# One block for projections, search and attention: splitting, rotation and search moved into the attention steps

## The chip, the cores and the metric

The kernel runs on one core of a Trainium2 chip. A time is device microseconds (us) of one execution, from launch to end. The profile comes from one profiled execution of its own; its span runs from the first instruction to the last.

## The reference

One decoder layer on 1024 tokens with 16 meta tokens in front of them (T = 1040), width 1024. All of it is float32.

```
proj = rms_norm(h) @ w_in                      # q,k,v of both attentions, index q,k,w, two gates
stick-breaking, 8 heads of 64, strictly causal:
  z = q k^T / 8;  log_not = -softplus(z);  a = exp(log_sigmoid(z) + sum of log_not over later keys);  o = a v
selected attention, 8 heads of 64, q and k rotated on their first 16 columns:
  score = sum over 8 index heads of relu(q_idx k_idx^T) * w_idx      # index q,k rotated on 8 of 32 columns
  the 256 highest-scored visible keys per query; softmax over them;  o = p v
merged = sigmoid(g_sb + b) * (o_sb @ w_branch_sb) + sigmoid(g_ds + b) * (o_ds @ w_branch_dsa)
h = h + rms_norm(merged @ w_out);  h = h + rms_norm(relu(rms_norm(h) @ w1)^2 @ w2)
```

## The kernel before

Every float32 matrix product is made of three reduced ones: each operand is split into `hi` (a copy in the fp32r type) and `lo` (what is left), and hi*hi, lo*hi and hi*lo are added in PSUM. Weights come in 123 units of 1024 x 128. For a unit, the SP queue loads `w_raw`, ACT makes `w_hi` (L120), POOL makes `w_lo` (L124), and PE multiplies 8 slices by 3 products over 1040 columns as three banks of 348, 348 and 344 columns, or over 1024 as two of 512 (`unit_mm`, L138).

The kernel is a row of blocks, with all engines meeting between them.

- **Norm** (L152 to L258): x is normalised, transposed and split into `x_hi`, `x_lo`.
- **Projections and search** (L345 to L675): 43 units, index units first, then 24 units of q, k, v and 16 of gates. ACT evacuates each (L425, L427, L475) and SP stores it unsplit to DRAM. Index rows come back, DVE rotates them (`rotate`, L557), they go out and come back four times over, ACT and POOL split them (L447, L494). From unit 9 on PE does one index head per unit between its slices (L548), through two one-bank buffers; ACT applies relu (L461) and DVE accumulates into `sc` (L588). Then DVE alone finds the 256th highest score of every query: 31 bits, highest first, and for each bit one counting pass over each of 7 key lengths (272 to 1040, L637), a comparison (L641) and a predicated copy (L644), and after it the mask `sel` (L655 to L675). PE multiplies the remaining units meanwhile. The q and k of the selected attention are rotated on DVE after the search, through DRAM.
- **Attention** (L722 to L1047): 128 jobs, one for each of 8 heads, 2 kinds and 8 blocks of 128 queries, with 144 to 1040 keys. They run as 4 turns of a hardware loop with 32 jobs each; a head of the stick-breaking kind (SB) and one of the selected kind (DS) alternate, longest block first. Operands come back from DRAM; DVE rounds q and k (L1034, L1035) and POOL makes their rest (L776, L778). A job: PE makes the logits (L824, L825, for SB also the mask, L827). SB: ACT takes two sigmoids (L901, L905), DVE scans (L980) and multiplies (L983). DS: DVE adds the mask and finds the extreme (L998), ACT takes the exponential (L908) and scales (L926). Then PE transposes the weights (L845), ACT rounds them (L920), DVE makes the rest (L1016), PE multiplies by v (L858), and ACT and DVE split the output (L932, L1029). Each engine's program fixes which job's part comes next; a job passes through some five of these steps.
- **Branches** (8 units), then **output product, norms and MLP**.

Of the kernel before, what the change touches and what calls it, by code (L numbers as in the profile page):

```python
# [7 lines left out]

# [35 lines left out]
U_IDX, U_QKV, U_GATE, U_BRANCH, U_OUT, U_MLP = 0, 3, 27, 43, 51, 59  # L44
# [13 lines left out]
R_V, R_K, R_Q = [0, 1536], [512, 2048], [1024, 2560]  # L58
R_GATE = 3072
# [7 lines left out]
O_MAIN = O_SEL + 2 * sum(KEYS)  # L67
O_RB = O_MAIN + 4 * NB * 1024


def key_chunks(n):

    return [(c, min(c + HALF, n)) for c in range(0, n, HALF)]


def build(nc, x, meta, w_units, b_gate, g_pre, g_post, g_mlp_pre, g_mlp_post, ident, strict, fill,
          rope_i, rope_d, out):
    with ExitStack() as ctx:
# [46 lines left out]

        def slot(base, i, k):

            return i * 2 + (base + k), (base + k) % 2, i + (base + k) // 2
# [132 lines left out]
        SB, DS = 0, 1  # L261
        O_RAW = O_MAIN + 2 * T * 4 + 2 * 8192
        q_raw = at("q_raw", [P, SEQ], F32, O_RAW)
        k_raw = at("k_raw", [P, T], F32, O_RAW + SEQ * 4)
        v_raw = at("v_raw", [DH, T], F32, O_RAW + (SEQ + T) * 4)
        unit_in = sem("a_in")

        def fetch(sp, hd, t):

            for half in range(2):  # L270
                sp.dma_start(q_raw[64 * half:64 * half + 64], proj[ds(hd * DH + R_Q[t], DH), META:T]).then_inc(unit_in, 16)
                sp.dma_start(k_raw[64 * half:64 * half + 64], proj[ds(hd * DH + R_K[t], DH), :]).then_inc(unit_in, 16)
            sp.dma_start(v_raw[:], proj[ds(hd * DH + R_V[t], DH), :]).then_inc(unit_in, 16)


        o = O_MAIN
        stage = at("stage", [P, 2, T], F32, o); o += 2 * T * 4
        qi_raw = at("qi_raw", [P, 2, SEQ], F32, o); o += 8192
        qi = at("qi", [P, 2, SEQ], F32R, o); o += 8192
        ki_raw = at("ki_raw", [P, T], F32, o); o += T * 4  # L280
        ki = at("ki", [P, T], F32R, o); o += T * 4
        relu_b = at("relu_b", [P, 2, HALF], F32, o); o += 4096
        sc = at("sc", [P, STOT], F32, o); o += STOT * 4
        junk2 = at("junk2", [P, 2, T], BF16, o); o += 2 * T * 2
        rp = [at(f"rope{n}", [P, T], F32, o + n * T * 4) for n in range(6)]
        o += 6 * T * 4
        rp_cos = at("rp_cos", [P, T], F32, o); o += T * 4
        rp_sin = at("rp_sin", [P, T], F32, o); o += T * 4
        w_tok = at("w_tok", [P, NB * HI], F32, o); o += 256
        w_t = at("w_t", [HI, SEQ], F32, o); o += SEQ * 4  # L290

        st_bits = at("st_bits", [P, 64], F32, o); o += 256
        assert o <= O_END, o
        sc_top = at("sc_top", [P, STOT], BF16, O_MAIN + 2 * T * 4)
# [3 lines left out]
        bit, need, thr = st_bits[:, 49:50], st_bits[:, 50:57], st_bits[:, 57:64]  # L298
# [10 lines left out]
        with ExitStack() as st:  # L309
# [22 lines left out]
            def _(sp):  # L332
# [19 lines left out]
                def stream(base, n, ahead=None):  # L352
                    with sp.Fori(0, n // 2) as i:
                        for k in range(2):
                            u, s, use = slot(base, i, k)
                            if ahead:
                                ahead(i, k)
# [1128 lines left out]
```

## Time and profile before

| | us |
|---|---|
| median of 3 runs | 2070.76 |
| lowest, highest | 2070.5, 2075.63 |
| the profiled execution | 2083.67 |
| its span | 2081.8 |
| PE busy | 1842.7 (89%) |
| DVE busy | 1106.9 (53%) |
| ACT busy | 700.2 (34%) |
| POOL busy | 465.1 (22%) |

The busy shares are averages over stages with different limits, so the span is cut into windows at the places where the work changes. "PEclk" is the TensorE clock that was granted, as a share of full speed. In a timeline, each row is the start, the time from the first start to the last end of the instructions merged in it, the engine, line, operation and tiles, and in brackets the idle time before it with what ended it.

### The profile page before, as it was taken

How to read it: one execution, taken by the hardware profiler on the slowest of the kernel's cores; microseconds unless marked ns; L12 is line 12 of the kernel's file. 1: busy time of each engine (PE TensorE's matmuls, PEld its weight loads, DVE VectorE, ACT ScalarE, POOL GpSimd, SP SyncE). 2: the span in 40 equal slices, each digit the busy share in tenths (PEclk: the TensorE clock that was granted, in tenths of full speed). 3: DMA queues.
4: the chain of work that ended last, by engine and by line, in shares of the span. 5: the costliest groups of instructions: out<-in, count | busy, mean ns of one | idle time of the engine just before them, and what ended most of it. 6: DMA issues, size and time to landing. Idle time of an engine off the chain costs nothing. (4 is left out here: it accounts for less than half of the span.)

```text
span 2081.8 us, 28389 instructions
## 1 busy us (share of the span) xinstructions
PE 1842.7 (89%) x10297; PEld 1573.4 (76%) x10297; DVE 1106.9 (53%) x1898; ACT 700.2 (34%) x1243; POOL 465.1 (22%) x186
## 2 busy tenths in 40 slices
PE   4988889999965877768778998999999999999997
PEld 3987889988754666656657786888888888888885
DVE  5106569999996768867778432442222222222226
ACT  4123442122113666656656413240302213021122
POOL 0124232122122202110111145021403214032230
PEclk7998889999987888878878999999999999999998
DMA  4232122242133121112212145321202112021123
GB/s 132 98 128 81 62 70 92 91 136 97 40 121 87 27 54 42 37 33 47 48 32 52 62 140 197 107 71 41 81 11 71 41 41 74 10 79 33 48 68 135
DMA packets 43405, 151.83 MB, mean 73 GB/s; under 512 B 6384, under 2 KB 6768, under 8 KB 43296
## 3 DMA queue, kind: packets, MB, share of 16 engines
q1 hardware_dynamic: 43296, 150.35, 23.1%
q8 instruction: 72, 1.18, 0.3%
q14 instruction: 37, 0.30, 0.1%
HBM read 117.81 MB, written 32.52 MB: 72 GB/s over the span
## 5 line engine op out<-in xcount | busy, mean ns | idle before, releaser
L138 PE MATMUL u_ps<-x_hi,w_hi 128*128 128x348 f32 (+1 forms) x904 | 226.1, 352 | 33.1 <-POOL w_lo L124 19.9
L124 POOL TENSOR_TENSOR w_lo<-w_raw,w_hi 128x1024 fp32r<-128x1024 f32 x53 | 129.2, 2439 | 477.7 <-ACT w_hi L120 477.7
L138 PE MATMUL u_ps<-x_lo,w_hi 128*128 128x348 f32 (+1 forms) x904 | 223.1, 348 | 0.0
L138 PE MATMUL u_ps<-x_hi,w_lo 128*128 128x348 f32 (+1 forms) x904 | 222.7, 348 | 0.0
L1339 ACT ACTIVATE relu<-bank 128x1024 f32<-128x1024 f32 x32 | 32.9, 1029 | 504.7 <-PE bank L1250 504.7
L1250 PE MATMUL bank<-m_hi,w_hi 128*128 128x512 f32 x512 | 199.5, 390 | 0.0
L1250 PE MATMUL bank<-m_hi,w_lo 128*128 128x512 f32 x512 | 199.2, 389 | 0.0
L1250 PE MATMUL bank<-m_lo,w_hi 128*128 128x512 f32 x512 | 199.2, 389 | 0.0
L138 PEld LDWEIGHTS u_ps<-x_hi,w_hi 128*128 128x128 f32 x904 | 163.9, 196 | 45.1 <-ACT stage L475 20.3
L845 PE MATMUL tp<-idf,a_buf 128*128 128x128 f32 (+1 forms) x704 | 124.3, 311 | 81.8 <-DVE pt_lo L1016 42.7
L1218 POOL TENSOR_TENSOR w_lo<-w_raw,w_hi 128x1024 fp32r<-128x1024 f32 x32 | 82.9, 2597 | 403.7 <-ACT w_hi L1315 403.7
L138 PEld LDWEIGHTS u_ps<-x_lo,w_hi 128*128 128x128 f32 x904 | 163.5, 196 | 11.9
L138 PEld LDWEIGHTS u_ps<-x_hi,w_lo 128*128 128x128 f32 x904 | 161.3, 193 | 11.4
L1420 DVE TENSOR_TENSOR acc<-acc,bank 128x1024 f32<-128x1024 f32 x56 | 68.3, 1220 | 188.4 <-PE bank L1226 187.6
L858 PE MATMUL o_ps<-pt_hi,v_hi 128*64 128x128 f32 (+1 forms) x704 | 159.2, 248 | 4.8 <-DVE o_lo L1029 3.5
L1407 DVE TENSOR_TENSOR sq<-relu 128x1024 f32<-128x1024 f32 x32 | 39.2, 1225 | 227.9 <-ACT relu L1339 227.9
L845 PEld LDWEIGHTS tp<-idf,a_buf 128*128 128x128 f32 (+1 forms) x704 | 78.5, 144 | 100.8 <-DVE pt_lo L1016 51.0
L1016 DVE TENSOR_TENSOR pt_lo<-tp,pt_hi 128x512 fp32r<-128x512 f32 (+3 forms) x224 | 121.8, 570 | 51.8 <-ACT pt_hi L920 50.4
L858 PE MATMUL o_ps<-pt_lo,v_hi 128*64 128x128 f32 (+1 forms) x704 | 149.1, 234 | 0.0
L858 PE MATMUL o_ps<-pt_hi,v_lo 128*64 128x128 f32 (+1 forms) x704 | 148.2, 233 | 0.0
L776 POOL TENSOR_TENSOR q_st<-q_raw,q_st 64x1024 fp32r<-64x1024 f32 x17 | 40.1, 2359 | 432.3 <-DVE k_hi L1035 432.3
L920 ACT CAST pt_hi<-tp 128x512 fp32r<-128x512 f32 (+3 forms) x224 | 104.3, 494 | 93.1 <-PE tp L845 92.8
(188 smaller groups left out, 3964.6 us busy)
## 6 DMA issues: line engine op xcount, KB each, us to landing
w_raw<-w_units SPq DMA_DIRECT2D x99, 512.0 KB, 3.5
proj<-stage SPq DMA_DIRECT2D x24, 520.0 KB, 2.7
raw<-w_units SPq DMA_DIRECT2D x24, 512.0 KB, 3.4
k_raw<-proj SPq DMA_DIRECT2D x34, 260.0 KB, 5.0
q_raw<-proj SPq DMA_DIRECT2D x34, 256.0 KB, 4.5
proj<-stage SPq DMA_DIRECT2D x16, 512.0 KB, 2.7
gate<-proj SPq DMA_DIRECT2D x16, 512.0 KB, 3.9
v_raw<-proj SPq DMA_DIRECT2D x17, 260.0 KB, 5.7
```

What stands on the lines that cost most here:

```text
L124: pool.tensor_tensor(w_lo[:, s], w_raw[:, s], w_hi[:, s].bitcast(F32), ALU.subtract).then_inc(lo_done, 1)
L138: mm = pe.matmul(o, w[:, s, kt, :], a[:, a_of(kt), c0:c1], start=(kt == kts[0] and n == 0), stop=(kt == kts[-1] and n == 2))
L776: pool.tensor_tensor(q_st[64:P, s], q_raw[64:P], q_st[64:P, s].bitcast(F32), ALU.subtract).then_inc(unit_lo, 1)
L845: mm = pe.transpose(tp[q][0:r, m * P:(m + 1) * P], a_buf[:, j % 4, c * P:c * P + r], idf[:])
L858: mm = pe.matmul(ops[s][0:DH, 0:P], v[0:r, t, c, :], w[0:r, s, c, :], start=(m == 0 and k_ == 0), stop=(m == len(tiles) - 1 and k_ == 2))
L920: act.copy(pt_hi[:, s, 4 * g:4 * g + m, :], tp[q][:, 0:m * P].rearrange("p (c k) -> p c k", c=m)).then_inc(rounded, 1)
L1016: dve.tensor_tensor(pt_lo[dst], tp[q][:, 0:m * P].rearrange("p (c k) -> p c k", c=m), pt_hi[dst].bitcast(F32), ALU.subtract).then_inc(b_fr ...
L1218: pool.tensor_tensor(unit_lo(v), raw_ring[(v - V0) % 3], unit_hi(v).bitcast(F32), ALU.subtract).then_inc(lo_done, 1)
L1250: mm = pe.matmul(m1_ps[n][:, c * HALF:(c + 1) * HALF], w[s][:, kt, :], a[:, kt, c * HALF:(c + 1) * HALF], start=kt == 0 and i == 0, stop=k ...
L1339: act.activation(relu8[:], m1_ps[n][:], ACT.Relu).then_inc(relu_done, 1)
L1407: dve.tensor_tensor(sq[:], relu8[:], relu8[:], ALU.mult).then_inc(sq_done, 1)
L1420: dve.tensor_tensor(acc[:, t], acc[:, t], m2_ps[g][:], ALU.add).then_inc(acc_done, 1)
```

## The change

- The projection block, the search and the attention block become one block, and their hardware loops become straight code. `CHUNK` lists 104 chunks: a unit's 348, 348 or 344 columns, or 512, each in one PSUM bank of its own pair.
- The rows of q and k are regrouped in the weights on the host, so that both halves of a rotation lie in one unit (`iA`, `rq`, `rk`). Rotation happens when such a chunk is evacuated: ACT copies it with its halves swapped, DVE multiplies twice and adds. Every q and k chunk is split at evacuation (ACT `stage_hi`, DVE `stage_lo`) and stored as hi and lo, so the rounding on ACT and DVE and the rests on POOL behind each reload go.
- 11 units are multiplied first, with the 8 index heads dealt between their slices (`INDEX_AT`) over four one-bank buffers. The other 32 units are dealt over the 64 SB jobs (`FILL`), by a table of costs that gives each step the same PE work.
- The attention steps run through all 64 SB jobs first and then all 64 DS jobs; blocks alternate between long and short (`BLOCKS`). The step of DVE holds two parts of the search (`SEARCH`): they are drawn from a generator, `select()`, that yields a cost in ns behind every instruction, until the sum of these has reached what the table has made due. The table shares 300,000 ns over 62 steps.
- The search reads the float32 scores in all 31 bits (before, the upper 15 bits came from a bf16 copy). The scan is done in place. The scaling by the softmax's sum moves from ACT (L926) to DVE (a `tensor_scalar`). Logits go to banks of at most 512 columns.
- SB outputs are stored to DRAM and come back, four pairs of heads, during the DS jobs (`RELOAD`), since `x_hi` and `x_lo` hold their place until then.
- In the branch block a gate is loaded as soon as its buffer is free, no longer behind the previous merge.

```diff
+BLOCKS = (7, 0, 6, 1, 5, 2, 4, 3)
+JOBS = [(t, H * t + h, i) for t in (SB, DS) for h in range(H) for i in BLOCKS]
...
+def work(j):
+    keys = [KEYS[JOBS[x_][2]] if 0 <= x_ < NJ else 0 for x_ in (j, j - 2, j - 3)]
+    return 0.89 * keys[0] + 0.9 * keys[1] + 1.41 * keys[2]
+
+def dve_work(j):
+    return (3.42 * KEYS[JOBS[j - 1][2]] if j >= 1 else 0) + (1.33 * KEYS[JOBS[j - 2][2]] if j >= 2 else 0) + 250
...
+cost_ = lambda n: 3 * (CHUNK[n][2] - CHUNK[n][1]) * 0.4435
...
+SEARCH_STEPS = STEPS - 2
+SEARCH_NS = 300e3
+dve_step = (SEARCH_NS + sum(dve_work(j_) for j_ in range(SEARCH_STEPS))) / SEARCH_STEPS
+SEARCH = [[max(0.0, dve_step - dve_work(j_)) / 2] * 2 if j_ < SEARCH_STEPS else [0.0, 0.0] for j_ in range(NJ + 4)]
+SEARCH[SEARCH_STEPS] = [1e8, 0.0]
...
             @block.tensor
...
+                for j in range(NJ + 3):
+                    if j < NJ:
+                        scores(j)
+                    for n, kt in FILL[j][0]:
+                        project(n, kt)
+                    if 2 <= j < NJ + 2:
+                        turn(j - 2)
...
+                    for n, kt in FILL[j][1]:
+                        project(n, kt)
+                    if j >= 3:
+                        product(j - 3)
...
             @block.vector
...
+                def select():
...
+                    for bit in reversed(range(BITS)):
+                        op(dve.tensor_scalar(cand.bitcast(I32), cur.bitcast(I32), 1 << bit, None, ALU.bitwise_or))
+                        yield 100
+                        settle()
+                        for j, b in enumerate(range(1, NB)):
+                            op(dve.tensor_scalar(sel[:, BOFF[b]:BOFF[b] + KEYS[b]], sc[:, blk(b)], cand[:, j:j + 1], None, ALU.is_ge, ALU.add,
+                                                 accum_out=cnt[:, j:j + 1]))
+                            yield 60 + 1.05 * KEYS[b]
+                        settle()
+                        op(dve.tensor_tensor(keep, cnt, thr_n, ALU.is_ge))
+                        yield 100
+                        settle()
+                        op(dve.copy_predicated(cur, keep.bitcast(I32), cand))
+                        yield 100
+                        settle()
...
+                for j in range(NJ + 4):
+                    if 4 <= j and JOBS[j - 4][0] == DS:
+                        rest_output(j - 4)
+                    if 1 <= j < NJ + 1:
+                        if JOBS[j - 1][0] == SB:
+                            stick(j - 1)
+                        else:
+                            normalise(j - 1)
+                    if j < NJ and JOBS[j][0] == DS:
+                        logits(j)
+                    if j < NJ + 3:
+                        for n in ENDS[j][0]:
+                            rest(n)
+                    due += SEARCH[j][0]
+                    while spent < due:
+                        spent += next(search, 1e9)
+                    if 2 <= j < NJ + 2:
+                        rest_weights(j - 2)
...
+                    due += SEARCH[j][1]
+                    while spent < due:
+                        spent += next(search, 1e9)
```

The first place is DVE in the search. Before, this is the loop's end, with nothing but the search in it (`sc` holds the scores, `st_bits` the bits, counts and thresholds):

```order
L637 TENSOR_SCALAR junk_364,st_bits<-sc,st_bits 128x784
L636 REGISTER_ALU
L637 TENSOR_SCALAR junk_364,st_bits<-sc,st_bits 128x912
L636 REGISTER_ALU
L637 TENSOR_SCALAR junk_364,st_bits<-sc,st_bits 128x1040
L639 TENSOR_SCALAR st_bits<-st_bits 128x1
L640 REGISTER_ALU
L641 TENSOR_TENSOR st_bits<-st_bits 128x7
L642 REGISTER_ALU
L644 COPY_PREDICATED st_bits<-st_bits 128x7
```

Now one step of DVE, in the fourth SB head (L949 and L952 are the scan and product of a job, L836 a chunk's `stage_lo`, L989 the rest of the transposed weights; L892, L896, L899 and L888 are the search):

```order
L949 SCALAR_TENSOR_TENSOR n_buf<-n_buf 128x528
L952 TENSOR_TENSOR a_buf<-a_buf,n_buf 128x528
L836 TENSOR_TENSOR stage_lo<-bk,stage_hi 128x512
L892 TENSOR_SCALAR sel,st_bits<-sc,st_bits 128x912
L892 TENSOR_SCALAR sel,st_bits<-sc,st_bits 128x1040
L989 TENSOR_TENSOR pt_lo<-bk,pt_hi 128x512
L989 TENSOR_TENSOR pt_lo<-bk,pt_hi 128x256
L896 TENSOR_TENSOR st_bits<-st_bits 128x7
L899 COPY_PREDICATED st_bits<-st_bits 128x7
L888 TENSOR_SCALAR st_bits<-st_bits 128x7
L892 TENSOR_SCALAR sel,st_bits<-sc,st_bits 128x272
L892 TENSOR_SCALAR sel,st_bits<-sc,st_bits 128x400
```

A bit's counts are now cut by the work of two jobs and a chunk, and one bit takes about a step.

The second place is where the search ends on DVE, in the step that holds the scan of job 45 (row one is its product; L940 is the last instruction of `select()`):

```order
L952 TENSOR_TENSOR a_buf<-a_buf,n_buf 128x400
L940 TENSOR_TENSOR sel<-sel,fill_f 128x128 x8
L989 TENSOR_TENSOR pt_lo<-bk,pt_hi 128x512
L989 TENSOR_TENSOR pt_lo<-bk,pt_hi 128x384
L949 SCALAR_TENSOR_TENSOR n_buf<-n_buf 128x656
L952 TENSOR_TENSOR a_buf<-a_buf,n_buf 128x656
L989 TENSOR_TENSOR pt_lo<-bk,pt_hi 128x512
L949 SCALAR_TENSOR_TENSOR n_buf<-n_buf 128x528
L952 TENSOR_TENSOR a_buf<-a_buf,n_buf 128x528
```

The search thus lies in steps 0 to 46 of the 64; in steps 47 to 63 DVE has only the jobs' own work.

The third place is PE in an attention step. Before (L845 transposes weights, L824 to L827 make logits, L858 multiplies by v):

```order
L845 MATMUL tp<-idf,a_buf 128x128 x7
L845 MATMUL tp<-idf,a_buf 16x128
L824 MATMUL z<-k_hi,q_st 128x400
L825 MATMUL z<-k_lo,q_st 128x400
L827 MATMUL z<-strict_b,idb 128x128
L858 MATMUL o_ps<-pt_hi,v_hi 64x128
```

Now (L647 multiplies by v, L622 to L625 make logits, L574 is a projection slice; `bk` are the eight PSUM banks):

```order
L647 MATMUL bk<-pt_hi,v_hi 64x128
L647 MATMUL bk<-pt_lo,v_hi 64x128
L647 MATMUL bk<-pt_hi,v_lo 64x128
L622 MATMUL bk<-k_hi_361,q_st_359 128x328
L623 MATMUL bk<-k_lo_363,q_st_359 128x328
L622 MATMUL bk<-k_hi_361,q_st_359 128x328
L623 MATMUL bk<-k_lo_363,q_st_359 128x328
L625 MATMUL bk<-strict_b,idb 128x128
L574 MATMUL bk<-x_hi,w_hi 128x348
```

Between the logits and the transposes of a step, and again behind the transposes, PE now has projection slices: 3 to 8 of them each time, in all 64 SB steps and in none of the DS steps.

## Rows read from the trace of the kernel before

**Rows 1.** Windows by stage: bounds, length, busy time of each engine, clock, DMA share.
```profile
45.00:150.00 105.00, 104.77 (x656) 104.49 (x656) 13.12 (x8) 16.96 (x25) 20.02 (x8) 0.98 0.35 115
150.00:161.00 11.00, 2.96 (x9) 2.53 (x9) 0.15 (x1) 4.29 (x6) 9.25 (x4) 0.56 0.12 48
161.00:305.00 144.00, 122.58 (x620) 114.79 (x621) 91.21 (x95) 60.48 (x123) 51.35 (x22) 0.84 0.24 74
305.00:628.00 323.00, 301.95 (x1541) 266.97 (x1539) 295.75 (x688) 68.31 (x81) 63.94 (x26) 0.97 0.27 95
628.00:643.00 15.00, 1.19 (x9) 0.94 (x9) 3.09 (x7) 1.78 (x4) 6.55 (x3) 0.54 0.49 124
643.00:1170.00 527.00, 406.63 (x3488) 340.04 (x3488) 397.16 (x815) 333.35 (x736) 86.01 (x33) 0.85 0.19 42
1170.00:2082.00 912.00, 886.16 (x3904) 730.29 (x3904) 282.32 (x248) 190.40 (x231) 223.11 (x86) 0.99 0.22 75
```

**Rows 2.** Timeline of PE: the first projection and the first branch product.
```profile
45.12 1.21 PE L138 MATMUL u_ps<-x_hi,w_hi 128*128 128x348 f32 x3 [6.31 <-PEq L147]
1170.53 0.72 PE L138 MATMUL br<-o_hi,w_hi 128*128 128x512 f32 x2 [1.49 <-PEq L722]
```

**Rows 3.** PE at full clock: two timeline rows, then one of the chain (start, length).
```profile
259.37 0.64 PE L138 MATMUL u_ps<-x_hi,w_hi 128*128 128x348 f32 x3
259.85 0.64 PE L138 MATMUL u_ps<-x_lo,w_hi 128*128 128x348 f32 x3
...
1411.57 43.77 PE bank L1226 x192
```

**Rows 4.** DVE in the index scores (timeline), and POOL's two groups beside it.
```profile
178.59 7.81 DVE L588 SCALAR_TENSOR_TENSOR sc<-relu_b,w_tok,sc 128x272 f32<-128x272 f32 x4 [2.99 <-ACT relu_b L461]
...
L124 POOL TENSOR_TENSOR w_lo<-w_raw,w_hi 128x1024 fp32r<-128x1024 f32 x53 | 129.2, 2439 | 477.7 <-ACT w_hi L120 477.7
L494 POOL TENSOR_TENSOR qi<-qi_raw,qi 32x1024 fp32r<-32x1024 f32 x16 | 39.1, 2443 | 1.7 <-POOL w_lo L124 1.0
```

**Rows 5.** Timeline of DVE in the search: its ends, and two bits.
```profile
313.44 1.50 DVE L597 TENSOR_TENSOR sc<-sc,fill_f 128x128 f32<-128x128 f32 x7 [0.29 <-DVE sc L588]
...
406.86 2.15 DVE L644 COPY_PREDICATED st_bits<-st_bits 128x7 f32<-128x7 int32 x1
409.39 0.17 DVE L632 TENSOR_TENSOR st_bits<-st_bits 128x7 int32<-128x7 int32 x1 [0.39 <-DVE st_bits L644]
...
415.75 0.17 DVE L644 COPY_PREDICATED st_bits<-st_bits 128x7 f32<-128x7 int32 x1
416.30 0.17 DVE L632 TENSOR_TENSOR st_bits<-st_bits 128x7 int32<-128x7 int32 x1 [0.39 <-DVE st_bits L644]
...
624.14 2.57 DVE L674 TENSOR_TENSOR sel<-sel,fill_f 128x128 bf16<-128x128 bf16 x8
```

**Rows 6.** DVE's groups for the jobs (count, busy us, mean ns, idle before), three by shape.
```profile
L1016 DVE TENSOR_TENSOR pt_lo<-tp,pt_hi 128x512 fp32r<-128x512 f32 (+3 forms) x224 | 121.8, 570 | 51.8 <-ACT pt_hi L920 50.4
L980 DVE TENSOR_TENSOR_SCAN c_buf<-n_buf 128x1040 f32<-128x1040 f32 (+3 forms) x64 | 98.2, 1534 | 31.2 <-ACT n_buf L905 30.9
L983 DVE TENSOR_TENSOR a_buf<-a_buf,c_buf 128x1040 f32<-128x1040 f32 (+3 forms) x64 | 66.1, 1033 | 2.2
...
L980 DVE TENSOR_TENSOR_SCAN c_buf<-n_buf 128x656 f32<-128x656 f32 x8 | 21.8, 2724 | 0.0
L980 DVE TENSOR_TENSOR_SCAN c_buf<-n_buf 128x784 f32<-128x784 f32 x7 | 12.5, 1781 | 0.0
L983 DVE TENSOR_TENSOR a_buf<-a_buf,c_buf 128x656 f32<-128x656 f32 x8 | 23.2, 2904 | 0.3
L983 DVE TENSOR_TENSOR a_buf<-a_buf,c_buf 128x784 f32<-128x784 f32 x7 | 6.8, 975 | 0.2
```

**Rows 7.** DVE scaling in place by a per-row scalar, 7 lengths of 272 to 1040.
```profile
L619 DVE TENSOR_SCALAR sc<-sc,st_bits 128x272 f32<-128x272 f32 (+6 forms) x7 | 3.9, 562 | 0.2
```

**Rows 8.** Waits in the attention stage: total us, times, longest.
```profile
ACT L900 <- PE z L827: 27.5, 3, 9.3
```

More of the change, by code:

```diff
@@ L9 @@
+import itertools
 from contextlib import ExitStack
@@ new lines, with even_chunks @@
+LO_NO = {n: k for k, n in enumerate(n for n in range(NC_ALL) if UNITS[CHUNK[n][0]][0] not in ("v", "g"))}
+CPU = {"iA": LAST_CHUNK[0] + 1}
+STORES = []
+for n_ in range(NC_ALL):
+    kind_ = UNITS[CHUNK[n_][0]][0]
+    dmas_ = {"iA": 8, "iC": 4, "rq": 4, "rk": 4, "v": 1, "g": 1}.get(kind_, 2)
+    STORES.append(dmas_ + (STORES[n_ - 2] if n_ >= 2 else 0))
+def even_chunks(keys):
+    n = -(-keys // HALF)
+    step = -(-keys // (2 * n)) * 2
+    return [(c * step, min((c + 1) * step, keys)) for c in range(n)]
@@ new lines @@
+STEPS = NJ // 2
+left_ = [(n_, k_) for n_ in range(NC_STEP, NC_ALL) for k_ in range(KT)]
+cost_ = lambda n: 3 * (CHUNK[n][2] - CHUNK[n][1]) * 0.4435
+per_step = (sum(cost_(n_) for n_, _ in left_) + sum(work(j_) for j_ in range(STEPS))) / STEPS
+FILL, due_, spent_ = [], 0.0, 0.0
+for j_ in range(NJ + 3):
+    parts_ = []
+    for part_ in range(2):
+        if j_ < STEPS:
+            due_ += (per_step - work(j_)) / 2
+        got_ = []
+        while left_ and j_ < STEPS and (spent_ < due_ or (j_ == STEPS - 1 and part_ == 1)):
+            got_.append(left_.pop(0))
+            spent_ += cost_(got_[-1][0])
+        parts_.append(got_)
+    FILL.append(parts_)
@@ L285, in build @@
[L285 to L294, printed above, removed]
+        stage_hi = at("stage_hi", [P, 2, HALF], F32R, O_STAGE)
@@ L520, in stream @@
-                def stream(base, n, outs, between=None):
-                    with pe.Fori(0, n // 2) as i:
-                        for k in range(2):
-                            u, s, _ = slot(base, i, k)
-                            unit(u, s, outs(s), before=between and (lambda kt: between(i, k, kt)))
-                for u in range(3):
-                    unit(u, u % 2, OUTS(u % 2))
-                stream(3, 6, OUTS)
-                pe.wait_ge(wt_in, 16)
-                for i in range(NB):
-                    mm = pe.transpose(sps[0][:, i * HI:(i + 1) * HI], w_t[:, i * P:(i + 1) * P], idf[0:HI, 0:HI])
@@ new lines, in logits @@
+                def logits(j):
+                    t, g, i = JOBS[j]
+                    s, keys = j % 2, KEYS[i]
+                    last = 3e38
+                    if j - 2 < NJ // 2:
+                        dve.wait_ge(a_done, j - 1)
+                    else:
+                        dve.wait_ge(exp_done, j - 1 - NJ // 2)
+                    for m, (c0, c1) in enumerate(ZCH[i]):
+                        z = Z_END[j] - len(ZCH[i]) + m
+                        dve.wait_ge(z_ready, z + 1)
+                        if m:
+                            dve.wait_ge(zd_used, z - NZ_SB)
+                        out = small[:, 16 + s:17 + s] if c1 == keys else small[:, 18 + m:19 + m]
+                        dve.tensor_tensor_reduce(n_buf[:, s, c0:c1], bk[(2 + z - NZ_SB) % 4][:, 0:c1 - c0], sel[:, BOFF[i] + c0:BOFF[i] + c1],
+                                                 -DH ** -0.5, last, ALU.add, ALU.min, out).then_inc(zd_used, 1)
+                        last = out
```

1380 lines of the change are left out of this document (676 added, 704 removed).

## The prediction

> **What bounds the kernel now.** I read the windows by stage first [rows 1]. Behind 1170 us PE is busy for 886 of 912 us at a clock of 0.99; nothing of the change reaches that part but the gate loads, which PE never waits for there. So everything lies between the first projection at 45.1 us and the first branch product at 1170.5 us [rows 2], 1125 us. The reader should see that no engine is full in them: PE is busy nearly throughout 45 to 150, but idle for 8 of the 11 us to 161, at 0.84 of the clock up to 305, and in the attention stage (527 us) PE is busy 77% at a clock of 0.85, DVE 75%, ACT 63%. From 305 to 628 PE and DVE are both near full: projections beside the search. The attention stage is bounded by hand-offs between three engines, the rest by PE or by DVE in turn. A merged stage can gain by filling PE's gaps with projections and DVE's with the search; what it cannot go below is the sum of work on the fuller engine.
>
> **PE's rates.** Three 348-column products start 0.48 us apart from the next three, so one takes 0.158; 192 products of 512 take 43.77, so 0.228 each [rows 3]. A unit of three banks is 72 x 0.158 = 11.4 us, one of two 48 x 0.228 = 10.9 us. Attention on PE is 406.6 us of busy time at 0.85 for 16 heads [rows 1]: 406.6 x 0.85 / 16 = 21.6 us a head at full clock, 2.7 us a job.
>
> **First 11 units with the index heads.** 7 units of three banks and 4 of two are 80 + 43 = 123 us. The 104 index products add about 0.2 us each, an estimate just above the 348-column price: 21 us. Before, a head took 20.5 us beside an 11.4 us unit, since POOL split q in two instructions of 2.44 us and DVE's accumulations stood still beside them: four of 272 columns took 7.81 us [rows 4]. That splitting now goes, and four buffers stand for two. What is late next is the first index operand: index q and k must go to DRAM and come back behind the first rotated chunk. Before, the same wait left PE idle 8 of 11 us and the clock at 0.56 [rows 1]; I take 12 us, and bound it by 0 and 20. Another 6 us are for the half clock at the start and the swap, two products and sum of each rotated chunk, which are longer than a copy. Sum 123 + 21 + 12 + 6 = 162 us. The sum of DVE here (104 accumulations, rotations, rests) is some 90 us over about 110, so it isn't the bound. Then 3 us to bring in the first head's v.
>
> **SB steps, DVE.** The order on DVE decides most. A bit of the search takes 416.30 - 409.39 = 6.91 us when nothing disturbs it [rows 5], so 31 take 214. Around them stay, for 7 lengths each, a scan (11.3 us, 98.2 less its holds over 8), two products as L983 (6.3 each), five scalings as L619 (3.9 each) [rows 6, 7], two counts (5.8 each, a bit less its small instructions) and 4 us of fills [rows 5]: 60. The search is 274 us, against 313 between its ends before [rows 5], which held the rotation and waits as well. But the table books its instructions by yields, and these add up to only 225 us (31 x 5.54, and 53 around). At 300 us booked over 62 steps the generator is empty in step 46, as the change's second order piece shows: the search is done in 47 steps, not 62. In those, DVE also has 47/64 of scans, products and half of the rests (98.2 + 66.1 + 60.9, less 23 of holds seen at 656 keys: 202 [rows 6]), 148 us, and the `stage_lo` of 10 units, 25 chunks at about 0.57 as L1016: 14. POOL makes 24 `w_lo` in them at 2.44 us [rows 4].
>
> The trace shows what such an instruction does to DVE: the predicated copy took 2.15 us against 0.17 [rows 5], the 656-key product 2904 ns where the longer 784-key one took 975 [rows 6], while the counting passes are never long. I count 1 us for each `w_lo`, since half or more find DVE in a counting pass or in PSUM work: 24 us; the bounds are 0 and 24 x 2.44 = 59. The Trainium skill (SBUF — State Buffer, section "Who interferes with whom") says that DVE with two SBUF inputs and a GpSimd instruction that reads SBUF exclude each other for a whole instruction, and that the counting form is free of it. By that rule the trace agrees, and the sum would go towards the upper bound only if every `w_lo` met such an instruction.
>
> 274 + 148 + 14 + 24 = 460 us. PE's share of these 47 steps: 32 units are 11 x 11.4 + 21 x 10.9 = 355 us over 64 steps, 5.55 a step, plus 2.7 for a job: 8.25 a step, 388 us, 84% of DVE's, so DVE is the bound. A transpose or product on PE needs DVE's half of an earlier step, a slack of about one step (10 us), so I put hand-off losses at 5%: 484 us, 10.3 a step.
>
> **SB steps 47 to 63** have no search. DVE has 3.2 us a step, PE 8.25: PE is the bound at full clock, 17 x 8.25 = 140, with 3% for the three-chunk blocks, where PE waits within a step: 145 us.
>
> **DS steps.** PE has no projections here. DVE's part: 397 us in all before, less 225 for the SB instructions, 172; the scaling that moves from ACT adds 8 heads of 4.3 us (L619's 3.9 and the shortest block) = 34, more and shorter logit pieces some 9, and the roundings of q and k go, some 23. That is 190 us, 3.0 a step. The step before was 527/128 = 4.1 us, and 3.9 without the 27.5 us of waits at the three turns of the loop [rows 1, 8]. The ring of waits is the same (scale, logits, exponential, next scale), with one engine change fewer. I take 3.8, nearer to the measured ring than to a full DVE: 243 us, bounds 190 and 264.
>
> **Outside.** Last three steps 5 us. From 1170.5 to the end, 911 us as before; the straight code costs nothing that I can see, since the MLP's straight code runs at 192 products in 43.77 us without a gap [rows 3]. The SB outputs' way over DRAM lies 6 steps behind and beside work; without that cover one trip would cost a few us. ACT has some 4 us a step in the SB part, under both others.
>
> **Sum.** 45 + 162 + 3 + 484 + 145 + 243 + 5 + 911 = 1998 us of span. The profiled execution lies 1.9 us above its span and 12.9 above the median of the runs, so 1998 + 1.9 - 12.9 = 1987 us, 4.0% below 2070.8.
>
> **Rivals.**
> *PE is the bound in all SB steps* (chance 0.15). If the search costs what the yields say, DVE's 460 becomes 411, close to PE's 388: 433 with losses, 51 less, 1936 us; if the holds vanish too, 1911. For it: waits on DVE's own semaphores may be hidden by the work between. Against: the 6.91 us hold only some 0.6 us of such waits.
> *POOL holds DVE in full* (0.13): 59 for 24 us, and a little in the index part, +37: 2024 us. For it: each step has a scan and product back to back, 3 us that are exposed. This is the outcome nearest to the skill's rule at its worst.
> *The ring of hand-offs sets the pace: slower* (0.15). All three SB and DS sums are of one full engine: 460 + 140 + 190 = 790 us, which I stretch to 872. Before, in the same ring, DVE was busy 397 of 499 us without the loop's turns, 0.80. If DVE waits at PE's transposes as it did then, because PE sits in a projection slice or waits for a bank, it is 790/0.80 = 990, 118 more: 2105 us. It decides from 956 us on, a busy share of 0.83. For it: the share before. Against: before, DVE had nothing else to do while it waited, and the table levels the steps.
> *TensorE falls to 1.2 GHz in the DS steps* (0.03): 2.7 us become 5.4 a step, over 3.8, +102: 2089 us, slower. Against: 0.85 before at a similar share of work.
> The forecast itself, 1960 to 2020, has 0.54.
>
> From no change a measurement tells 0.3% here, 6 us. Faster: 0.54 + 0.15 + 0.13, and little of the rest, 0.82; slower 0.15; the same 0.03. The range of 8 in 10 goes from 1920, inside the first rival, to 2085, inside the slower ones.
>
> **What would show it.** DVE over 90% busy in the first two thirds of the SB steps, at some 10 us a step, with the last mask fill (the `sel` sum with `fill_f`) near 695 us; from there PE over 95% busy at clock 1 to about 840 us; DS steps of 3.6 to 4 us with DVE 75 to 85% busy; the first branch product near 1087 us. The index part ends near 210 us with one PE gap of about 10 us behind the first rotated chunk. I am wrong if DVE is below 85% busy before the last fill (the ring), if the fill comes before 650 us (PE the bound), or if the DS steps take more than 4.2 us.

## The result and the profile after

The changed kernel takes 2053.24 us (median of 4 runs, 2052.47 to 2053.39), the kernel before in the same job 2070.70: a ratio of 0.991, with a 95% interval of 0.989 to 0.993. It is faster by 0.9%, where 4.0% was forecast: 66 us more than the 1987 us of the prediction, above the 1960 to 2020 of the forecast itself.

The windows of the changed kernel, cut at the stages that the prediction names (length, busy time of PE, PEld, DVE, ACT and POOL with their instructions, granted clock, DMA share, GB/s; PEld is PE's weight load, and the DMA share is the mean busy share of the 16 DMA engines), answer to [rows 1]:

```profile
45.00:121.00 76.00, 60.51 (x314) 54.44 (x315) 22.39 (x42) 21.95 (x44) 9.59 (x4) 0.91 0.40 129
121.00:258.00 137.00, 95.94 (x497) 87.70 (x495) 70.20 (x115) 55.15 (x120) 15.17 (x7) 0.86 0.36 107
258.00:743.00 485.00, 416.08 (x2627) 363.46 (x2628) 435.09 (x849) 166.42 (x381) 61.26 (x24) 0.91 0.31 89
743.00:893.00 150.00, 144.80 (x901) 118.15 (x900) 56.25 (x72) 62.50 (x138) 19.70 (x9) 1.00 0.30 89
893.00:1142.00 249.00, 199.64 (x1747) 173.28 (x1745) 181.83 (x549) 131.39 (x330) 1.77 (x1) 0.88 0.25 62
1142.00:2051.00 909.00, 884.02 (x3904) 729.09 (x3904) 284.44 (x249) 190.54 (x232) 223.19 (x86) 0.99 0.23 75
```

The bounds come from its timelines: PE brings in the first head's v (the index stage is over), DVE writes the last mask fills, PE starts the branch (start, length; these answer to [rows 2] and the last row of [rows 5]):

```profile
257.99 0.73 PE L597 MATMUL bk<-idf,v_raw 64*128 64x64 f32 x9 [2.46 <-issue]
...
741.24 1.70 DVE L940 TENSOR_TENSOR sel<-sel,fill_f 128x128 bf16<-128x128 bf16 x8
...
1142.78 0.70 PE L253 MATMUL br<-o_hi,w_hi 128*128 128x512 f32 x2 [0.94 <-PEq L409]
```

| stage | forecast | measured |
|---|---|---|
| up to the first projection | 45 | 45 |
| first 11 units with the index heads, first v | 165 | 213 |
| SB steps with the search | 484 | 485 |
| SB steps behind it | 145 | 150 |
| DS steps and the last three | 248 | 250 |
| branch to the end | 911 | 909 |

One stage is off by 48 us, all others together by 6 net. DVE is 90% busy while it searches (435 of 485 us), PE 97% at full clock behind the search, a DS step takes 3.9 us. So the question is narrow: what holds the index stage? In it PE is idle for 56.6 of 213 us, and the waits of 121 to 258 us name the cause of the largest part (total us, times, longest):

```profile
PEld bk L585 <- DMA qi<-iq_d: 37.9, 5, 19.0
PE bk L585 <- DMA qi<-iq_d: 36.2, 5, 18.7
ACT stage_hi L705 <- DMA q_d<-stage_lo: 8.8, 3, 3.7
ACT w_hi L239 <- DMA w_raw<-w_units: 7.6, 1, 7.6
ACT stage_hi L712 <- DMA k_d<-stage_lo: 6.9, 4, 3.0
```

The q of an index head comes late five times. SP issues these loads in one queue with the stores (SPq; issue start, and the time that the issue itself took):

```profile
136.63 0.48 SPq L467 DMA_DIRECT2D k_d<-stage_lo  x1
...
141.45 4.42 SPq L479 DMA_DIRECT2D qi<-iq_d  x2
...
146.49 4.56 SPq L467 DMA_DIRECT2D k_d<-stage_lo  x1
151.09 4.29 SPq L234 DMA_DIRECT2D w_raw<-w_units  x1
...
219.75 7.15 SPq L465 DMA_DIRECT2D q_d<-stage_lo  x1
```

An issue of 0.48 us becomes one of 4 to 7 (a row with x2 holds two, or more than one with the time between them). Two readings offer themselves. **Theory A**: the loads are placed too late, behind stores and with only two q buffers. **Rivals**: the stage is slow for another reason, and q is merely where it shows.

### The profile page after: what moved, and what is told of

The parts are those of the page before. It is cut to its first block and busy times, and to the rows that moved or that the text cites. A ratio compares the mean times of both kernels' runs of the same rounds, so it can differ in the third digit from the quotient of the medians.

```text
span 2051.5 us, 25668 instructions
## 1 busy us (share of the span) xinstructions
PE 1817.6 (89%) x10056; PEld 1539.7 (75%) x10056; DVE 1074.3 (52%) x1911; ACT 652.7 (32%) x1283; POOL 335.5 (16%) x135
## 5 line engine op out<-in xcount | busy, mean ns | idle before, releaser
L574 PE MATMUL bk<-x_hi,w_hi 128*128 128x512 f32 (+2 forms) x832 | 321.8, 387 | 10.6 <-PEq L262 6.3
L574 PE MATMUL bk<-x_lo,w_hi 128*128 128x512 f32 (+2 forms) x832 | 309.4, 372 | 0.0
L574 PE MATMUL bk<-x_hi,w_lo 128*128 128x512 f32 (+2 forms) x832 | 308.0, 370 | 0.0
L574 PEld LDWEIGHTS bk<-x_hi,w_hi 128*128 128x128 f32 x832 | 167.1, 201 | 29.2 <-POOL w_lo L243 6.4
L892 DVE TENSOR_SCALAR_CACHE_REDUCE sel<-sc,st_bits 128x272 bf16<-128x272 f32 (+6 forms) x217 | 183.2, 891 | 1.0
L574 PEld LDWEIGHTS bk<-x_hi,w_lo 128*128 128x128 f32 x832 | 166.1, 200 | 18.6
L574 PEld LDWEIGHTS bk<-x_lo,w_hi 128*128 128x128 f32 x832 | 166.9, 201 | 13.8
L989 DVE TENSOR_TENSOR pt_lo<-bk,pt_hi 128x512 fp32r<-128x512 f32 (+2 forms) x224 | 121.2, 571 | 102.4 <-ACT pt_hi L753 101.8
L647 PE MATMUL bk<-pt_hi,v_hi 128*64 128x128 f32 (+1 forms) x704 | 161.8, 252 | 0.2 <-DVE pt_lo L989 0.2
L647 PE MATMUL bk<-pt_lo,v_hi 128*64 128x128 f32 (+1 forms) x704 | 149.6, 235 | 0.0
L647 PE MATMUL bk<-pt_hi,v_lo 128*64 128x128 f32 (+1 forms) x704 | 149.0, 234 | 0.0
```

Source lines behind the costliest of these rows:

```text
L574: mm = pe.matmul(pj[b][:, 0:c1 - c0], w[:, s, kt, :], a[:, kt, c0:c1], start=kt == 0 and k == 0, stop=kt == KT - 1 and k == 2)
L647: mm = pe.matmul(ops[j % 2][0:DH, 0:P], v[0:r, g % 2, c, :], w[0:r, j % 2, c, :], start=m == 0 and k == 0, stop=m == len(tiles) - 1 and k ...
L892: op(dve.tensor_scalar(sel[:, BOFF[b]:BOFF[b] + KEYS[b]], sc[:, blk(b)], cand[:, j:j + 1], None, ALU.is_ge, ALU.add, accum_out=cnt[:, j:j ...
L989: dve.tensor_tensor(pt_lo[dst], tp[n % 2][:, 0:m * P].rearrange("p (c k) -> p c k", c=m), pt_hi[dst].bitcast(F32), ALU.subtract).then_inc( ...
```

## The experiments

The kernel before had medians of 2070.7 to 2076.1 us in the five sessions of measurement. A difference of under some 5 us between runs of two sessions is therefore no finding by itself; where the text reads a small one, it goes by places inside the traces.

**e1_ring3: a third q buffer.** Each load is issued one head earlier.

```diff
-QI_AT = {... if any(m_ >= (h_ - 1) * NCH + 1 ...)) for h_ in range(2, HI)}
+QI_AT = {... if any(m_ >= (h_ - 2) * NCH + 1 ...)) for h_ in range(3, HI)}
...
-        qi = at("qi", [P, 2, SEQ], F32R, O_A + 8 * T + 4096)
+        qi = [at(f"qi{s}", [P, SEQ], F32R, O_A + 8 * T + 4096 + 4096 * s) for s in range(2)]
+        qi.append(at("qi2", [P, SEQ], F32R, O_QK + QK_SET))
...
```

> Changed kernel with a third buffer for the index q, so that SP issues the load of head h one head earlier (first product of head h-2 in place of h-1). Theory A (the loads of index q come too late because SP issues them in order behind stores and a two-buffer ring leaves them a lead of less than one head): the waits of PE for qi go from 48 us in six gaps to the first one alone, 10 to 13 us, the index stage from 213 to about 175 us, and the time from 2053 to about 2017 us. Rival B (the stage is long because of slower matmuls and rotation, and the waits only show where slack sits): the gaps move to other waits, and the time stays above 2040. Rival C (SP's issues, stretched to 4 to 9 us, hold the whole stage back, stores and weights too): half of the gain, 2030 to 2040, with w_raw or stage waits in place of qi.

2053.4 us (2050.9 to 2054.9): nothing gained. Its waits from 90 to 258 us:

```profile
PEld bk L586 <- ACT relu_b L722: 43.5, 13, 11.4
...
PE bk L586 <- ACT relu_b L722: 39.4, 12, 11.1
ACT stage_hi L706 <- DMA q_d<-stage_lo: 29.4, 4, 9.5
ACT stage_hi L713 <- DMA k_d<-stage_lo: 25.6, 6, 7.2
...
PE bk L586 <- DMA qi<-iq_d: 11.6, 1, 11.6
```

PE waits for q once, as forecast, and for ACT instead. ACT waits 55 us for stores of q and k to land, to get its stage buffer back; the ReLUs of the index products stand behind that eviction on ACT, and PE's next products behind the ReLUs. PE's waits for both add up to what they were: 39.4 + 11.6 = 51 us here, 47.9 for q and 5.0 for ACT in the changed kernel from 45 to 258 us. Theory A has fallen. What rival B names as its sign has come, though the ground that it gives (slower matmuls, rotation) is not the cause, as e5 and e6 show.

**e2_actq: the q loads issued by ACT.**

```diff
-                        for h in range(2, HI):
-                            if QI_AT[h] == n:
-                                sp.wait_ge(s_ready, (h - 1) * NCH)
-                                load_qi(h)
...
+                    h = m // NCH + 2
+                    if m % NCH == NCH - 1 and h < HI:
+                        if h == 2:
+                            act.wait_ge(ki_in, 64)
+                        for g in range(2):
+                            act.dma_start(qi[64 * g:64 * g + 64, h % 2].bitcast(F32), iq_d[h]).then_inc(qi_in[h % 2], 16)
```

> Changed kernel with the index q loads of heads 2 to 7 issued by ACT, right behind the ReLU of the last product of head h-2, in place of SP; still two buffers. Theory A (SP's order is the cause): the loads land a head before they are needed, as with three buffers, and the time is 2015 to 2025 us; ACT's twelve issues add at most 12 x 0.6 = 7 us. If the transfers themselves are slow (rival C), qi keeps waits of 5 us or more per head and ACT's issues are stretched too: above 2035.

2052.2 us (2051.2 to 2055.8), with 29.1 and 20.3 us of ACT's waits for the same stores. Leaving SP's queue doesn't help either.

**e3_noload: q of heads 2 to 7 not loaded.**

> Changed kernel without the loads of index q for heads 2 to 7: these heads use the q of heads 0 and 1, so the scores are not the reference's. It is the bound of what any placing of these loads can give. Theory A: 2010 to 2018 us, PE idle for qi once. Rival B: above 2040.

2048.7 us (2045.6 to 2052.5). Without any of these loads only 5 us go (the last mask fill comes 4 us earlier). What the loads waited for is still there, and this trace, with less traffic in it, shows it plainly. SP's queue, then windows at the same place (the last two columns are the DMA share of 16 engines and GB/s):

```profile
164.06 2.51 SPq L465 DMA_DIRECT2D q_d<-stage_hi  x1
166.61 5.00 SPq L465 DMA_DIRECT2D q_d<-stage_lo  x1
171.66 4.98 SPq L234 DMA_DIRECT2D w_raw<-w_units  x1
```

```profile
160.00:165.00 5.00, 1.90 (x12) 1.61 (x11) 0.69 (x1) 0.99 (x2) 0.00 (x0) 1.00 0.13 47
165.00:170.00 5.00, 3.86 (x14) 3.86 (x15) 3.88 (x4) 2.69 (x6) 2.37 (x1) 0.66 0.13 51
170.00:175.00 5.00, 2.48 (x17) 2.19 (x15) 0.65 (x2) 0.22 (x1) 0.00 (x0) 1.00 0.13 51
```

The share stands at 0.13 = 2/16, window after window, at some 50 GB/s, while transfers queue up. It looks as if two engines carried everything; the trace has no row for a single DMA engine, so this is read from the share. The stores that are in flight there are those of the q and k units, and in the order of SP's instructions they are the ones with an outer dimension of 2 (the head pair), where a weight load has 128 rows:

```order
102 L234 DMA w_raw<-w_units 128x1024
103 L465 DMA q_d<-stage_hi 2x64x512
104 L465 DMA q_d<-stage_lo 2x64x512
```

A 256 KB store at 50 GB/s takes 5.2 us, and a q chunk has two of them: 10.5 us for a chunk that PE projects in 24 x 0.228 = 5.5 us [rows 3], and some five index products of 0.2. With k it is 2 x 3.6 us against 24 x 0.158 = 3.8 and the same 1. So the stores fall behind, and ACT finds its buffer still in flight. This is **theory D**, and the next two runs test it. The Trainium skill ("DMA: Bandwidth & Descriptors", section "Why a DMA increments its semaphore by 16 and not by 1") states that the number of engines is the largest up to 16 that divides the slowest dimension of both sides. The share of 2/16 agrees with it.

**e5_split: one store for each head of the pair.** Bytes and rows stay.

```diff
-                            sp.dma_start(q_d[2 * p:2 * p + 2, half, :, q0:q1], src[:, 0:w]).then_inc(stored[s], 16)
+                            for e in range(2):
+                                sp.dma_start(q_d[2 * p + e, half, :, q0:q1], src[64 * e:64 * e + 64, 0:w]).then_inc(stored[s], 16)
```

(and the same for k_d)

> Changed kernel with each store of a q or k unit to the scratch in DRAM given as two transfers of 64 rows (one for each head of the pair) in place of one of 2x64 rows; bytes and rows (1392 and 2048 bytes) are as before, SP has twice as many issues there. Theory D (a transfer whose outer dimension is 2 is carried by 2 of the 16 DMA engines: the DMA share stands at 0.13 and 50 GB/s while such stores run, so a 256 KB store takes 5 us; two stage buffers then hold ACT's evictions, and behind them the index ReLUs and PE): no stretch at a share of 0.13 is left in the index stage, the waits of ACT for DMA q_d and k_d stores (some 13 us in the changed kernel, 55 us with a third q buffer) go under 5 us, SP's issues stay under 2 us, the stage falls from 213 to about 175 us and the time to 2005 to 2020 us. Rival E (the rows of 1392 bytes, or the doubled bytes, cost it): no more than 8 us gained, waits as before.

**e6_layout: the hi/lo half outermost in DRAM**, so that a store is 128 equal rows and no transfer is added to it.

```diff
-        q_d, k_d = scratch("q_d", 2 * H, 2, DH, SEQ), scratch("k_d", 2 * H, 2, DH, T)
+        q_d, k_d = scratch("q_d", 2, 2 * H, DH, SEQ), scratch("k_d", 2, 2 * H, DH, T)
-                            sp.dma_start(q_d[2 * p:2 * p + 2, half, :, q0:q1], src[:, 0:w]).then_inc(stored[s], 16)
+                            sp.dma_start(q_d[half, 2 * p:2 * p + 2, :, q0:q1], src[:, 0:w]).then_inc(stored[s], 16)
-                    sp.dma_start(q_st[s][:].bitcast(F32), q_d[g]).then_inc(q_in[s], 16)
+                    for half in range(2):
+                        sp.dma_start(q_st[s][64 * half:64 * half + 64].bitcast(F32), q_d[half, g]).then_inc(q_in[s], 16)
```

> Changed kernel with the scratch for q and k laid out with the hi/lo half outermost, so that a store of a unit is one transfer of 128 equal rows in place of 2x64; q of a head is loaded as two transfers of 64 rows in place of one of 128. Same number of store issues as before. Theory D: as e5_split, 2000 to 2020 us, a few us under it since SP issues less. Rival E: no change.

e5_split takes 1998.9 us (1998.0 to 2000.7) and e6_layout 2000.1 us (1996.9 to 2001.8), ratios to before 0.964 (0.962 to 0.966) both: 53 to 54 us gained by the shape of a transfer alone, somewhat more than expected of e5 (2005 to 2020). Rival E (row length, bytes) is out, since both were kept. Windows of e6_layout at its stage bounds, and SP's queue at the place of the stretched issues:

```profile
45.00:215.00 170.00, 148.91 (x810) 136.90 (x811) 93.66 (x156) 77.76 (x163) 24.84 (x12) 0.96 0.47 144
215.00:691.00 476.00, 414.57 (x2627) 361.84 (x2627) 435.30 (x848) 167.02 (x381) 62.22 (x24) 0.92 0.32 90
691.00:840.00 149.00, 143.80 (x896) 117.15 (x894) 56.04 (x72) 61.97 (x138) 19.10 (x8) 1.00 0.31 88
840.00:1090.00 250.00, 201.05 (x1754) 174.55 (x1751) 182.16 (x549) 131.85 (x332) 2.38 (x1) 0.88 0.27 63
```

```profile
150.72 0.32 SPq L465 DMA_DIRECT2D q_d<-stage_hi  x1
151.45 0.32 SPq L465 DMA_DIRECT2D q_d<-stage_lo  x1
151.81 1.09 SPq L479 DMA_DIRECT2D qi<-iq_d  x2
```

The index stage falls from 213 to 170 us (forecast 165), and the SB steps with the search from 485 to 476; the others stay. PE is busy for 148.9 us there, against 60.5 + 95.9 = 156.4 with as many products: so of the 43 us, 36 are idle time of PE, and 7 are products at the lower granted clock, 0.91 and 0.86 where it is now 0.96. The waits of PE for q are 13.3 us in two places, and ACT waits for no store of q or k in either run. Transfers of another shape profit as well. Loads in the index stage from 131 us on, the changed kernel first (KB each, median us from issue to landing):

```profile
w_raw<-w_units SPq DMA_DIRECT2D x7, 512.0 KB, 12.7
qi<-iq_d SPq DMA_DIRECT2D x10, 256.0 KB, 9.3
```

and e6_layout:

```profile
w_raw<-w_units SPq DMA_DIRECT2D x7, 512.0 KB, 3.9
qi<-iq_d SPq DMA_DIRECT2D x10, 256.0 KB, 4.2
```

**e13_half: the narrow shape kept, half the bytes.** It asks whether a narrow store costs by its length against the chunk, or by being in the queue at all.

```diff
-                            if kind in ("v", "g"):
+                            if kind in ("v", "g") or (kind in ("q", "k") and u < U_STEP):
                                 break
...
-                    sp.dma_start(q_st[s][:].bitcast(F32), q_d[g]).then_inc(q_in[s], 16)
+                    lo = 0 if g < 4 else 1
+                    for half in range(2):
+                        sp.dma_start(q_st[s][64 * half:64 * half + 64].bitcast(F32), q_d[g, half * lo]).then_inc(q_in[s], 16)
...
-                        sp.dma_start(k_lo[s][64 * half:64 * half + 64].bitcast(F32), k_d[g, 1]).then_inc(q_in[s], 16)
+                        sp.dma_start(k_lo[s][64 * half:64 * half + 64].bitcast(F32), k_d[g, lo]).then_inc(q_in[s], 16)
```

> Changed kernel with the stores still 2x64 rows, but in the first 11 units the lo halves of the q and k units not stored; the loads of heads 0 to 3 read the hi halves in their place, so those heads' scores are not the reference's. A chunk of q then has one store of 5.1 us on two engines against a chunk of 5.7 us, one of k 3.5 against 5. Theory D as throughput (a chunk's stores on two engines must take longer than the chunk to hold ACT): the stage ends near 218 us, time 2010 to 2020 us, since the 2x64 stores of the SB steps stay. Rival F (one narrow transfer already holds what is queued behind it, weights and index q, whatever its length against a chunk): stage end at 235 or later, time over 2030.

2020.6 us (2019.8 to 2022.5), and the index stage ends here:

```profile
223.80 0.73 PE L601 MATMUL bk<-idf,v_raw 64*128 64x64 f32 x9 [1.97 <-issue]
```

That is 34 of the 43 us between 258.0 and 214.9, and ACT waits for no store of q or k any more: length against the chunk is most of it. The other 9 are rival F, in small: from 45 us on PE waits 21.8 us for q, 8.5 more than in e6_layout. The division isn't sharp, since half the bytes also hold the queue for half the time, so a part of the 34 may belong to F; no run separates them further.

**e11_v264: v made narrow too**, in the kernel of e7 below, by a padding row in the scratch.

```diff
-scratch("v_d", 2 * H, DH, T)
+scratch("v_d", 2 * H, DH + 1, T)
...
-sp.dma_start(v_d[2 * p:2 * p + 2, :, c0:c1], ...)
+sp.dma_start(v_d[2 * p:2 * p + 2, 0:DH, c0:c1], ...)
...
```

> e7_layout_even (1947 us) with the scratch of v padded by a row, so that each v store is 2x64 rows in place of 128: same bytes and rows. Theory D by dose: a v chunk has one store of 174 KB, which two engines at 50 GB/s carry in 3.5 us, less than the 5 us of a chunk. So the trace shows the share of 0.13 and 50 GB/s again while v stores run alone, with no loss at all in time beyond 5 us: the width decides only where a chunk's stores take longer than the chunk (two of 256 KB, 10 us against 5.7). If the time rises by over 15 us, the transfers behind the stores in the queue matter more than their own length.

1955.0 us (1954.1 to 1955.2) against 1947.4: 7.6 us slower, over the 5 I allowed, far under 15. The index stage ends at 221.9 us where it ends at 214.3 in e7, so all of it lies there. The window and the wait that it brings back:

```profile
175.00:180.00 5.00, 3.33 (x14) 3.33 (x15) 1.86 (x4) 0.97 (x3) 0.00 (x0) 0.73 0.13 45
```

```profile
PE bk L586 <- DMA qi<-iq_d: 5.2, 2, 3.3
```

One store of 3.6 us in a chunk doesn't hold the stage buffers, but q behind it in the queue comes late. Here the second part of the cost stands by itself: no store of v is waited for, and only what is queued behind it comes late.

**e4_even: the search spread over all 62 steps.** It tests the other large claim of the forecast, DVE the bound for 47 steps and PE behind them.

```diff
-SEARCH_NS = 300e3
+SEARCH_NS = 227e3
```

> Changed kernel with SEARCH_NS at 227e3 in place of 300e3, the sum of what the search books, so that it is spread over all 62 steps and does not end in step 47. DVE busy in the SB steps 435 + 56 = 491 us, PE about 528 at full clock. If the 485 us up to the search's end were bound by DVE and the 147 us behind it by PE, as forecast, both now share 64 steps of about 9 us: SB ends some 50 us earlier, time about 2000 us (1985 to 2020). Rival (the ring of hand-offs sets the pace when both are full): less than 15 us gained, above 2038.

2011.5 us (2006.2 to 2011.8): 42 us gained, the low side of what was expected. **e7_layout_even** joins it with e6_layout.

> e6_layout and SEARCH_NS at 227e3 (the search over all 62 steps). If the two gains add up (about 40 us each, one in the index stage and one in the SB steps): 1965 to 1980 us; the evictions of projections in the SB steps may give a few more. If they are the same gain: not under 2000.

1947.4 us (1945.8 to 1948.3), ratio 0.939 (0.937 to 0.941), under the 1965 to 1980 expected: the two gains add up to 95 us, 53 and 42, and 106 came. The traces show where the rest can lie: from 258 to 850 us of e4_even ACT still waits 45 us for narrow stores of q and k, and in the SB steps of e7 for none. Windows of its SB steps, where PE is now nearly full in every one:

```profile
214.00:400.00 186.00, 169.96 (x1082) 149.73 (x1083) 153.15 (x319) 67.86 (x159) 24.71 (x10) 0.95 0.41 114
400.00:600.00 200.00, 191.95 (x1318) 170.44 (x1317) 183.74 (x357) 83.51 (x190) 31.60 (x12) 0.99 0.31 90
600.00:780.00 180.00, 172.78 (x1074) 140.55 (x1074) 157.91 (x244) 74.06 (x163) 25.65 (x10) 1.00 0.34 93
```

**e8_split_even_ring3** adds the third q buffer, to e5_split.

> e5_split, SEARCH_NS at 227e3, and the third buffer for index q of e1_ring3. If the loads of index q come late again once the stores no longer hold the stage, the third buffer gives 5 to 15 us beyond e7_layout_even; if not, the same time within 4 us.

1945.6 us (1944.0 to 1948.0), the same as e7 within their spread: with wide stores the q loads are in time.

**e9_nopool: POOL's `w_lo` left out in the SB steps**, in e6_layout; the stale w_lo makes the projections of these units others than the reference's.

```diff
+                    pool.wait_ge(hi_done, v + 1)
+                    pool.memset(small[:, 400 + v:401 + v], 0.0).then_inc(lo_done, 1)
```

> e6_layout (2000 us, last mask fill at 689 us) with POOL's part w_lo left out for the units of the SB steps but the last two before the branch: POOL writes one column instead and signals as before, so w_lo of these units is stale and the output is not the reference's. It measures the term 'POOL holds DVE for 1 us a w_lo', 24 us in the first 47 steps. If the term is right: last fill near 665 us, time 1972 to 1982 us. If a w_lo holds DVE for its full 2.44 us: fill near 630 to 640, time near 1950. If POOL's work costs DVE nothing: 1996 to 2001.

1968.6 us (1968.2 to 1969.7), 31.5 us less than e6_layout and just under the 1972 to 1982 expected for my term, and the last fill 32 us earlier (30 counted from the start of the SB steps), from 689.4 us to:

```profile
657.68 1.70 DVE L946 TENSOR_TENSOR sel<-sel,fill_f 128x128 bf16<-128x128 bf16 x8
```

DVE's busy time in these steps falls by 34 us, from 435.3 to 401.5. A `w_lo` thus costs it 1.3 to 1.4 us (30/24 and 34/24), between my 1 and the full 2.44. Scans and products of the jobs, in e6_layout and then here (count, busy us, mean ns), show half of it:

```profile
L950 DVE TENSOR_TENSOR_SCAN n_buf<-n_buf 128x1040 f32<-128x1040 f32 (+7 forms) x46 | 69.0, 1500 | 0.0
L953 DVE TENSOR_TENSOR a_buf<-a_buf,n_buf 128x1040 f32<-128x1040 f32 (+7 forms) x46 | 47.8, 1040 | 1.6
```

```profile
L955 DVE TENSOR_TENSOR_SCAN n_buf<-n_buf 128x1040 f32<-128x1040 f32 (+7 forms) x46 | 63.7, 1384 | 0.0
L958 DVE TENSOR_TENSOR a_buf<-a_buf,n_buf 128x1040 f32<-128x1040 f32 (+7 forms) x46 | 35.7, 775 | 1.6
```

The other half lies in four passes of the search that don't count (23 us, 14 here) and in its small instructions on seven columns (18 us, 10 here). The 217 counting passes take 183 us in both, and `pt_lo` 41.6 in both.

**e10_later: index products two chunks later**, in e7.

```diff
-slots_ = [... for k_ in range(KT)][2:]
+slots_ = [... for k_ in range(KT)][18:]
```

> e7_layout_even (1947 us) with the first index product two chunks later (18 slots of the table skipped in place of 2), so that the 104 products stand in 142 slots. The one gap of 11.7 us at PE for the first index operand, with the clock at half behind it, should go: 8 to 15 us gained, 1932 to 1939 us. Rival: the denser products make DVE (93 us busy of 169 in this stage, 76 of the last 100) or a late load of q the bound there, and give it back: within 4 us of 1947.

1938.8 us (1931.8 to 1942.3): about 9 us gained, a wide spread; the index stage ends at 202.4 us in place of 214.3. The one gap of 11.7 us is gone; four short ones have come:

```profile
PE bk L586 <- DMA qi<-iq_d: 5.7, 4, 2.9
```

**e12_normact: the DS scaling back on ACT**, in e7.

> e7_layout_even (1947 us) with the scaling of the DS weights by ACT, as in the kernel before, in place of DVE: DVE loses 34 us of its 184 in the 64 DS steps (254 us), ACT's 135 rise by some 40. If the ring of waits sets the 3.9 us step, as forecast (DVE 73% busy): within 8 us either way, one hand-off more being against it. If DVE sets it: 15 to 30 us faster.

1944.6 us (1944.4 to 1945.6), 2.7 us less, which is no finding. DVE loses 25 us of its busy time in the DS steps (184.4 to 159.4 from 780 to 1034 us) and they hardly move: DVE doesn't set them. With PE busy for 81% of them and ACT for 69%, the ring of waits is left, as forecast.

**e14_best** holds e6_layout, e4_even, e10_later, e1_ring3 and e12_normact.

> The parts that gained, together: scratch with the half outermost, SEARCH_NS 227e3, index products two chunks later, three buffers for index q, DS scaling on ACT. e10_later left PE 5.7 us of waits for index q in the dense stage, which the third buffer should take; the scaling on ACT gave 2.7 us. 1928 to 1936 us if they add up.

1927.6 us (1925.0 to 1931.9), ratio to before 0.929 (0.927 to 0.930): 7.1% faster than the kernel before and 6.1% than the changed one. PE waits for q once, 2.8 us. Its stages:

```profile
45.00:198.50 153.50, 146.32 (x808) 135.86 (x808) 91.64 (x156) 77.39 (x163) 24.37 (x11) 0.98 0.52 159
198.50:773.00 574.50, 543.80 (x3524) 468.22 (x3525) 497.16 (x919) 229.20 (x519) 81.76 (x33) 0.98 0.35 98
773.00:1018.50 245.50, 196.89 (x1750) 171.09 (x1748) 156.66 (x486) 172.37 (x394) 2.23 (x1) 0.89 0.27 64
```

## Why the prediction was wrong, point by point

**The index stage, 165 us, was the step that failed.** The prediction adds PE's work, the first index operand and the half clock, and says of DVE that it isn't the bound; the stores of q and k have no term in the sum, neither their length on the DMA engines nor their hold on SP's queue, and no reason is given for that. The stage took 213. What was counted was sized well: the gap was 11.7 us for 12, and with wide stores the whole stage needs 170 us, 5 over the forecast. The 43 us between are the narrow stores, which e5 and e6 take away: some 34 for stores that together take longer than their chunk, some 9 for loads behind them in the queue (e13, where the division isn't sharp). What was missing is a length for each store: bytes and count alone (2 x 256 KB a chunk, at the 115 GB/s of the first window of before [rows 1]) make 4.6 us, shorter than a chunk; with the shape, 2x64 rows where a weight load has 128, it is 10.5. None of the three signs that the prediction names for being wrong has come (DVE below 85%, the fill before 650 us, DS steps over 4.2 us): all three watch the steps behind this stage. And that 2053 us lies inside its range of 8 in 10 is luck, since none of the rivals that fill that part of the range is what happened.

**The first gap behind the first rotated chunk** was right in size, 11.7 us, and e10 takes it away.

**SB steps with the search, 484 us**: measured 485, but errors cancel. The work was put at 460 us, 24 of them POOL's holds, and the losses at 24; DVE was busy 435 us, holds included, and idle 50. The holds were too small by 10 (34 in e9, taken from e6_layout, which is busy as long), the rest of the work so some 35 too large, and the losses too small by 26, of which 9 are the narrow stores (485 to 476 in e6_layout). A part of the 35 is only booked elsewhere: by the prediction's own 0.6 us of waits in a bit, an estimate, 31 bits hold 19 us that its work counts and the trace has as idle time. That the bound is DVE, and that the table runs out of search in step 46, is confirmed by e4: the same instructions spread over 62 steps give 42 us, 53 once the stores are wide (1947.4 against 2000.1). The first rival (PE the bound in all SB steps) is not what this change did; it is what e7 does.

**SB steps behind the search** (145, measured 150) and **DS steps** (248, measured 250) were right, PE at full clock in the first, the ring in the second; e12 shows that DVE isn't the bound there, and the ring follows by what is left. The rival of a ring that stretches all steps (2105 us) has fallen: DVE was 90% busy in the search. That of POOL's full hold (59 us) has fallen too, with 30 to 34 in its place. The rival at half clock hasn't come: 0.88 in the DS steps.

**The conversion.** I took 12.9 us off since the profiled execution of before lay that far above its median. The profiled one of the changed kernel lies on its median (span 2051.5, median 2053.2), so 13 of the 66 us are this subtraction. Nor was it the profiler: of the 30 later executions of the kernel before, four took 2083 us or more. Which instructions of before were slower in that one execution, and whether the stages that stay had any of it, no run tells; it stays open.

The sum of the misses: 48 + 1 + 5 + 2 - 2 in the stages and 13 in the conversion is 67, for 66.

## What to carry to other kernels

Read the shape of each transfer as the queue sees it, and compare the length of all stores of a chunk with the chunk: an outer dimension of 2 gave a DMA share that stands at 0.13, that of 2 engines in 16, and 50 GB/s, and another order of the scratch in DRAM mended it at no cost. When a late load heads the list of waits, take the load away (e3) before placing it better; here the wait only changed its name. And a table that books work should book what the work adds up to, or one engine is full first and another later.

## What the runs showed of the hardware

A single DMA issue on SP takes 0.3 to 0.8 us from 45 to 216 us of e5_split and e6_layout, but up to 7.6 us in the same stage of the changed kernel, where narrow transfers are in flight; the issuing queue, not only the landing, is held. So narrow stores delay wide transfers behind them: a weight load of 512 KB landed after 12.7 us in place of 3.9. Why an issue waits, no run shows. Two transfers of 64 rows did as well as one of 128 (1998.9 and 2000.1 us). And a POOL subtraction of 2.6 us beside a DVE with scans and products costs DVE 1.3 to 1.4 us on average (e9), less than its length: the counting passes (183 us in both runs) and the rests that read PSUM (41.6 us in both) lose nothing to it.
